# Queueing attention's steps by estimated times instead of one per weight pair, in a two-block transformer kernel

## The reference

```
mod = silu(c) @ w_ada + b_ada            # 2048 -> 12288: six vectors of 2048
h   = modulate(rmsnorm(x), shift_m, scale_m)
dq, dk, dv, q_lat, kv_lat, k_pe = split(h @ w_in)
o_diff = softmax(q1 k1) v - lam * softmax(q2 k2) v      # 8 heads, then an rmsnorm per head
o_mla  = softmax(q_nope k_nope + q_rope k_rope) v       # 8 heads, q and k,v from latents
x = x + gate_m * (concat(o_diff, o_mla) @ w_out)
x = x + gate_f * (relu(modulate(rmsnorm(x), shift_f, scale_f) @ w_ff1)**2 @ w_ff2)
x = rmsnorm(x)
# second block
hn @ w_in_2 -> q,k,v,z of 12 sliding-window heads, of 12 forgetting heads, q,z of 4 memory heads, 3 gates
mk, mv = rmsnorm(mem) @ w_mem_kv
y = sum over branches of sigmoid(gate) * ((attention * silu(z)) @ w_branch)
out = x + y @ w_out_2
```

## Time and profile before

| | before |
|---|---|
| median of 3 runs (lowest, highest) | 2119.35 us (2119.01, 2122.26) |
| the profiled execution: its time | 2116.66 us |
| its span | 2114.6 us |
| PE busy | 1980.5 us, 94% |
| PEld busy | 1631.5 us, 77% |
| DVE busy | 1315.1 us, 62% |
| ACT busy | 941.6 us, 45% |
| instructions | 24917 |

### The profile page before, as it was taken

One profiled execution on the slowest core, in us unless ns is written; L12 is line 12 of the kernel. 1 busy time (PEld: TensorE's weight loads), 2 busy tenths in 40 slices (PEclk: granted clock), 3 DMA queues, 4 the chain that ended last, 5 costly groups with the idle time before them and its releaser, 6 DMA issues. The chain is left out here.

```text
span 2114.6 us, 24917 instructions
## 1 busy us (share of the span) xinstructions
PE 1980.5 (94%) x9272; PEld 1631.5 (77%) x9272; DVE 1315.1 (62%) x2079; ACT 941.6 (45%) x1436; POOL 129.4 (6%) x94
## 2 busy tenths in 40 slices
PE   6798896869899999999999999989999999999999
PEld 3377775548778888888888878889998788888887
DVE  3888776788796555555555556567665555545554
ACT  2554445434544344444434455455444444444442
POOL 0000000002000110110010022010000001101000
PEclk9899998979999999999999999999999999999999
DMA  9997675759797555555555545534544456656654
GB/s 361 382 376 263 241 254 187 249 188 343 273 356 267 194 200 188 190 192 184 191 191 188 186 160 182 188 112 144 164 134 145 132 159 199 189 189 196 192 189 169
DMA packets 128969, 448.83 MB, mean 212 GB/s; under 512 B 14289, under 2 KB 14545, under 8 KB 128337
## 3 DMA queue, kind: packets, MB, share of 16 engines
q1 hardware_dynamic: 124928, 433.74, 60.4%
q0 software_dynamic: 1568, 7.34, 0.9%
q10 hardware_dynamic: 2352, 6.17, 0.8%
HBM read 443.00 MB, written 4.19 MB: 211 GB/s over the span
## 5 line engine op out<-in xcount | busy, mean ns | idle before, releaser
L1724 DVE TENSOR_TENSOR wlo<-raw,whi 128x1024 fp32r<-128x1024 f32 (+4 forms) x554 | 659.4, 1193 | 593.4 <-ACT whi L1511 568.4
L1511 ACT ACTIVATE whi<-raw 128x1024 fp32r<-128x1024 f32 (+4 forms) x554 | 557.0, 1007 | 708.2 <-PE g L1386 638.4
L1381 PE MATMUL g<-whi,lhsA_hi 128*128 128x512 f32 (+4 forms) x1840 | 713.6, 389 | 27.7 <-issue 13.7
L1382 PE MATMUL g<-whi,lhsA_lo 128*128 128x512 f32 (+4 forms) x1840 | 693.5, 379 | 0.0
L1386 PE MATMUL g<-wlo,lhsA_hi 128*128 128x512 f32 (+4 forms) x1840 | 463.7, 374 | 0.0
L1381 PEld LDWEIGHTS g<-whi,lhsA_hi 128*128 128x128 f32 x1840 | 354.9, 193 | 91.9 <-issue 33.1
L1382 PEld LDWEIGHTS g<-whi,lhsA_lo 128*128 128x128 f32 x1840 | 354.9, 193 | 53.3 <-issue 1.7
L1386 PEld LDWEIGHTS g<-wlo,lhsA_hi 128*128 128x128 f32 x1840 | 339.2, 190 | 54.6
L1381 PE MATMUL g<-whi,lhsF_hi 128*128 128x512 f32 x512 | 200.6, 392 | 0.0
L1382 PE MATMUL g<-whi,lhsF_lo 128*128 128x512 f32 x512 | 199.4, 389 | 0.0
L1729 DVE SCALAR_TENSOR_TENSOR raw<-raw,srow 128x1024 f32<-128x1024 f32 x147 | 178.0, 1236 | 19.2 <-DMA raw<-in_w_ada 19.0
(11 more groups left out here) (270 smaller groups left out, 1559.4 us busy)
## 6 DMA issues: line engine op xcount, KB each, us to landing
raw<-in_w_ff SPq DMA_DIRECT2D x182, 512.0 KB, 3.6
raw<-in_w_in SPq DMA_DIRECT2D x161, 512.0 KB, 3.9
raw<-in_w_ada SPq DMA_DIRECT2D x147, 512.0 KB, 5.1
region<-in_w_ff SPq DMA_DIRECT2D x74, 512.0 KB, 4.1
raw<-in_w_out SPq DMA_DIRECT2D x60, 512.0 KB, 5.1
raw<-in_w_in SPq DMA_DIRECT2D x80, 384.0 KB, 3.1
region<-in_w_ada SPq DMA_DIRECT2D x34, 512.0 KB, 5.9
region<-in_w_in SPq DMA_DIRECT2D x15, 512.0 KB, 7.9
```

Of the source, the lines that this page charges most:

```text
L1381: eng.matmul(o, p.xh[:, kk, t * P:t * P + P], h, start=p.first and kk == 0, stop=False)
L1382: eng.matmul(o, p.xl[:, kk, t * P:t * P + P], h, start=False, stop=False)
L1511: eng.activation(p.hi, p.raw, ACT.Copy).then_inc(p.hi_done[0], 1)
L1724: eng.tensor_tensor(p.lo, p.raw, p.hi.bitcast(F32), ALU.subtract).then_inc(p.lo_done[0], 1)
```

## The change

The planner keeps an estimate of the time of each engine (`now`) and of each mark, that is each semaphore value that a step sets (`due`). `TAKES` gives for every kind of step its engine and its us; `step()` adds them. A generator now yields the engine and the marks that its next step waits for; `pump()` lets it go on when those marks are due by the time at which that engine, or PE, is estimated to be (`soon`), and goes round the generators until none moves. Where the planner must have something (`idle`), the generator with the earliest marks goes ahead. The parts of a head are cut by engine: `diff_exp` becomes `diff_max` and `diff_exp`, `diff_mix` becomes `diff_recip`, `diff_scale` and `diff_mix`, `diff_out` loses `diff_sq`; in the same way `soft_max`, `causal_recip` and `x_gain_sq` are split off. The table `ADA_LEFT` is gone: `fill()` queues dots as long as DVE's estimated time at the end of the next one is within `AHEAD` of PE's (3.0 us for the first 64 dots, 3.5 for the next 96, 2.0 for the rest). No instruction is added or dropped in the arithmetic.

```diff
+AHEAD, SLACK = (3.0, 3.5, 2.0), 0.0
...
-ADA_LEFT = {22: 157, 23: 156, 24: 155, 25: 152, 26: 151, 27: 150, 29: 149, 30: 148, 31: 147, 33: 146, 34: 145, 35: 144,
...
+TAKES = {
...
+    "diff_scores": (("pe", 1.15, 6),), "diff_max": (("dve", 0.9, 5),), "diff_exp": (("act", 1.1, 9),),
+    "diff_recip": (("dve", 0.45, 3),), "diff_scale": (("act", 0.45, 5),), "diff_mix": (("dve", 0.46, 5),),
...
+    "mla_scores": (("pe", 1.7, 7),), "soft_max": (("dve", 0.9, 6),), "soft_exp": (("act", 1.1, 8),),
...
+    "store_out": (), "ada_sum": (("dve", 0.6),)}
...
+    due = {landed[n]: t for n, t in dict(c=7.0, cst=9.0, cols=10.0, m0=17.0, m1=20.0, pos=22.0, rows=22.0, x0=26.0, x1=27.0,
+                                         x2=29.0, x3=30.0, xr=0.0, gfin=0.0).items()}
+    now = dict(sp=0.0, dma=9.0, pe=12.0, act=20.0, dve=10.0, pool=0.0)
...
+    def take_time(engine, us, marks, *made):
+
+        now[engine] = max([now[engine]] + [due[m] + 0.07 for m in marks if m in due]) + us
+        for m in made:
+            due[m] = now[engine] + 0.1
 
     def step(*s):
         order.append(s)
+        kind = s[0] + "_pool" if s[0] in ("heads_scale", "add_rows", "y_add") and s[-2] == "pool" else s[0]
+        for engine, us, *at in TAKES.get(kind, ()):
+            take_time(engine, us, marks_in(s[1:]), *[s[i] for i in at])
...
         while all(b.busy for b in ring):
-            pump(1, 4)
+            pump(1, 4, True)
         return pick(ring)
...
+        now["sp"] = max([now["sp"]] + [due[m] for m in raw_free[i]]) + 0.05
+        now["dma"] = max(now["dma"], now["sp"] + 2.0) + n * 0.00282
         raw_free[i] = None
+        due[raw_sem[i], raw_count[i]] = now["dma"]
...
+        take_time("act", 0.1 + 0.00167 * n, [p.landed] + [p.after] * bool(p.after), p.hi_done)
...
         step("ada", x, t, b, k0 // 2, done, b.after)
+        take_time("dve", 1.15, [t], done)
...
     def fill():
-        state["turn"] += 1
-        left = ADA_LEFT.get(state["turn"], 999)
-        while len(adas) > left:
+        while adas:
+            i = state["slot"] % state["ring"]
+            if raw_free[i] is None or (state["hold"] and adas[0][0] >= 20):
+                break
+            issue = max([now["sp"]] + [due[m] for m in raw_free[i]])
+            arrival = max(issue + 2.0, now["dma"]) + 1.45
+            if max(now["dve"], arrival) + 1.2 > now["pe"] + AHEAD[0 if adas[0][0] < 8 else 1 if adas[0][0] < 20 else 2]:
+                break
             ada_next()
 
     bg, started, counts, t_of = deque(), set(), {}, {}
 
-    def pump(n=1, width=2):
+    waiting = {}
+
+    def soon(g, slack):
+
+        engine, marks = waiting.get(id(g)) or ("pe", ())
+        return max([due[m] for m in marks] + [0.0]) <= max(now[engine], now["pe"]) + slack
+
+    def advance(g):
...
+        if w == "end":
+            bg.remove(g)
+        else:
+            waiting[id(g)] = w
+        return len(order) > at or w == "end"
+
+    def pump(n=1, width=2, idle=False):
         for _ in range(n):
             fill()
-            live = 0
-            for g in list(bg):
-                if live < width or g in started:
-                    started.add(g)
-                    live += 1
-                    if next(g, "end") == "end":
-                        bg.remove(g)
+            moved, again = False, True
+            while again:
+                again, live = False, 0
+                for g in list(bg):
+                    if live < width or g in started:
+                        started.add(g)
+                        live += 1
+                        if soon(g, SLACK):
+                            again = advance(g) or again
+                moved = moved or again
+            if idle and not moved:
+                held = [g for g in bg if g in started and waiting.get(id(g))]
+                held.sort(key=lambda g: max([due[m] for m in waiting[id(g)][1]] + [0.0]))
+                for g in held:
+                    if advance(g):
+                        break
...
-                pump(1, 3)
+                pump(1, 3, True)
...
+            if p.native:
+                take_time("pe", 3.43, [p.landed, p.ready, *p.free], tok)
+            else:
+                take_time("pe", 8 * (0.013 + n / 2400), [p.hi_done, p.ready, *p.free])
+                take_time("pe", 4 * (0.013 + n / 2400), [p.lo_done], tok)
...
+        yield "pe", bs[0].after + bs[1].after + [t_of["qT", j], t_of["kT", j]]
         tok = mark("scored")
         step("diff_scores", h, [b.ap for b in bs], bs[0].after + bs[1].after, t_of["qT", j], t_of["kT", j], tok)
-        yield
+        yield "dve", [tok]
+        kms = []
+        for c, b in enumerate(bs):
+            kms.append(mark("negmax"))
+            step("diff_max", c, b.ap, m.ap, [tok] + m.after, kms[c])
         pb = yield from grab(PB)
         for c, b in enumerate(bs):
-            km, ke = mark("negmax"), mark("exp")
-            step("diff_exp", c, b.ap, m.ap, s.ap, pb.ap, tok, m.after, s.after, pb.after, km, ke)
+            yield "act", [kms[c]]
+            ke = mark("exp")
...
-        yield
-        kr, kt = mark("recip"), [(mark("scaled"), mark("mixed")) for _ in range(2)]
...
+        yield "dve", [ke]
+        kr = mark("recip")
+        step("diff_recip", s.ap, ke, kr)
+        kms = []
+        for t in range(2):
+            yield "act", [kr]
+            kms.append(mark("scaled"))
+            step("diff_scale", t, s.ap, pb.ap, kr, kms[t])
+        for t in range(2):
+            yield "dve", [kms[t]]
+            kt = mark("mixed")
+            step("diff_mix", t, s.ap, pb.ap, kms[t], kt)
+        s.release(kt)
...
-        yield
+        yield "act", [tok]
         k = copied(T, tok, pt.ap[:, :], 512, 1.0, *pt.after)
         O = yield from grab(OB)
+        yield "pe", O.after + [k, t_of["dv", j]]
...
-        yield
-        k, ka = mark("odiff"), mark("sqd")
-        step("diff_out", odiff[j][:, :, P * hh:P * hh + P], O.ap, 8 * j + hh, tok, stage, k, ka)
+        yield "dve", [tok]
+        k = mark("odiff")
+        step("diff_out", odiff[j][:, :, P * hh:P * hh + P], O.ap, tok, stage, k)
+        yield "act", [k]
+        ka = mark("sqd")
+        step("diff_sq", O.ap, 8 * j + hh, k, ka)
         O.release(ka)
...
     def diff_end(j):
         yield from need(("ssd", j), 4)
+        yield "dve", [t_of["ssd", j]]
         k = mark("rms")
         step("diff_rsqrt", j, t_of["ssd", j], k)
-        yield
+        yield "dve", [k]
         k2 = mark("odn")
```

More of the change, by code:

```diff
@@ L404, in ada_next @@
             step("ada_sum", c, b, done)
+            due[ada_done[c]] = now["dve"] + 0.1
             b.after = [ada_done[c]]
@@ L950, in reload @@
         step("load_xr", fence())
+        due[landed["xr"]] = max(now["pe"], now["act"], now["dve"]) + 8.0
         x_tok.extend([landed["xr"]] for _ in range(4))
@@ L1024, in final_chunk @@
     def final_chunk(j):
-        for _ in range(2 * (j == 3)):
-            yield
         for p in range(2):
@@ L1296, in turn_y @@
     def turn_y(y, ks, j):
-        for _ in range(2):
-            yield
         for p in range(2):
+            yield "pe", ks
             b = yield from grab(SB)
+            yield "pe", b.after
             tok = turned(b, blocks_of(y.ap, (2 * p * P, 2 * p * P + P)), *ks)
-            yield
+            yield "act", [tok]
             split_from(b, tok, 2, [0.5, 0.5], lhs_y, 4 * j + 2 * p, *stage)
-            yield
         y.release(tok)
@@ L1608, in _ @@
             elif kind == "soft_exp":
-                _, bank, mcol, scol, pb, scale, _, _, s_after, pb_after, km, t = s
-                for m in (km, *s_after, *pb_after):
+                _, bank, mcol, scol, pb, scale, after, km, t = s
+                for m in (km, *after):
                     w.wait_ge(*m)
@@ L1862, in _ @@
                 ins.then_inc(t[0], 1)
-            elif kind == "diff_exp":
-                _, c, bank, mcol, _, _, tok, m_after, _, _, t, _ = s
-                for m in (tok, *m_after):
+            elif kind == "diff_max":
+                _, c, bank, mcol, after, t = s
+                for m in after:
                     w.wait_ge(*m)
```

219 lines of the change are left out of this document (136 added, 83 removed), and 8 rows, old and new, of the table ADA_LEFT.

## The result

| | before | after |
|---|---|---|
| median of 4 runs (lowest, highest) | 2119.18 us (2118.41, 2122.26) | 2053.02 us (2050.08, 2055.5) |
| ratio, 95% interval | | 0.9685 (0.9668 to 0.9701) |
| span of the profiled execution | 2114.6 us | 2048.2 us |
| span less PE's busy time | 134.1 us | 86.5 us |
| granted clock | 0.975 | 0.983 |

The change takes 66 us off. The direction was right and the size was not.

A forecast was written before the change was run, and what follows sets the result against it. PE was taken as the bound, busy 1980.5 of 2114.6 us, leaving 134.1 us idle. Terms +2 - 6 - 20 + 0 - 4 - 2 - 8 = -38 gave 2081 us, range 2060 to 2115.

The forecast's parts named there:

- the clock's price for the heads: Heads in 237 to 404 us: 33 us at the lower clock, called mostly idle time or its wake; -2 us taken.
- -19 for idle time: Heads in 237 to 404 us: of 28.7 us of PE idle, all but 3.7 and 6 us would go.
- I give half back: Second block, 1225 to 1735 us: 14.8 us of waits go, but packed causal heads return half; -8 us.
- +2 to +3.6: Pairs 16 to 46: two to three uncovered dots ahead of low parts for pairs 18 and 19 cost this many us.
- Start: Transposes moved ahead of the first native delay it by 0 to 3.5 us; +2 us taken.
- Heads 4 to 7: 404 to 485 us: dots cluster with head steps on DVE, 86% busy; 0 us taken, bounds -25 to +37.
- fourth case: Pairs 63 to 102: dots ahead of head steps on DVE make it slower, 2136 us; chance 0.10.
- sign of being wrong: The forecast fails if PE's waits for DVE's mixed probabilities or ACT's exps grow; no size given.
- larger gain: Heads in 404 to 485 us gain like the earlier ones, 20 to 40 us more: 2040 to 2062 us; chance 0.08.
- 16 us that the text itself works out for the clock: Heads in 237 to 404 us: at most another 16 us would go if all low-clock time ran high.
- second case: 237 to 485 us: DVE is the bound, gaps only move, the -20 is lost: 2101 us; chance 0.13.
- The third: Planner's estimates are off, such as high parts booked at 0.955 against 1.07 us; waits stay, 2115 to 2120 us; chance 0.03.

The follow-up runs named there:

- e9: Kernel after the change, PE made to wait for 2, 3 or 5 chained GpSimd operations, at lone pairs and in series of 12 pairs: 2330.1 us.
- e6: Kernel after the change, PE made to wait for one GpSimd operation after five lone pairs and each of pairs 600 to 629: 2104.6 us.
- e7: Kernel after the change, memory's arrival and engines' first times re-estimated, mostly later, and the arrival awaited by name: 2045.0 us, ratio 0.965.
- e8: Kernel after the change, dots behind pairs 98 to 103 allowed only within 0.0 us of PE's time in place of 3.5: 2067.6 us, ratio 0.975.
- e11: Kernel after the change, dots 65 to 160 let through within 8.0 us of PE's time in place of 3.5: 2103.3 us, ratio 0.993.
- e13: e7's kernel, steps held until 1.0 us after their marks are estimated due: 2086.0 us; the next run let them through 1.0 us before: 2096.5 us.
- e15: e7's kernel, a high part booked at 1.07 us in place of 0.955: 2058.2 us, ratio 0.971.
- e2: Kernel before the change, with the time estimate added but used for the dots alone, heads moved and cut as before: 2125.8 us, ratio 1.003.
- e5: Kernel after the change, but with as many dots queued behind every pair as the kernel before had by then: 2096.3 us, ratio 0.988.
- e3: Kernel after the change, heads' steps cut as before in place of by engine: 2086.2 us, ratio 0.984.
- e1: Kernel after the change, dots placed by the old table of dots left per turn, which bunched them: 2133.9 us, ratio 1.007.

## Why the prediction was wrong

Its place of the gain was right in every stretch for which it had one, and its size was short by a factor of 1.7: 28 us are missing, 15 of them in PE's busy time (-18.8 for -3.7) and 13 in its idle time (-47.6 for -34.3). By its steps:

- The failing step is the clock's price for the heads. From the earlier trace rows it had 33 us at the lower level, called them "most of it idle time or its wake" and took "-2 for it". Idle time was 1.9 us of it: PE was busy in 30.1 of the 32.0 us that the trace has, and by the two levels half of that, 15 us, was paid. After, 3.2 us at the lower level are left, which makes -13.5 for the -2. With the moved matmuls, some 3 us, this is the 16.6 that busy time lost in pairs 64 to 91. The -19 for idle time there was nearly right (-21.7).
- The same price was left out elsewhere. In the second block PE was busy at the lower level for 12.5 us before and 3.4 after, 4.6 of the 8.0 us that busy time lost there; the other 3.4 have no cause shown. At the feed-forward's start 9.5 us went for 4.3 us of waits; of the 5.2 in busy time 1.7 are the clock (3.4 us at the lower level before, none after) and some 2 the matmuls that moved. Over the whole program PE was busy at the lower level for 76.7 us before and 49.5 after, so 13.6 of the 18.8 us are the clock. e9 shows the price by itself. A wait that the profile shows as 2.3 us costs 4.2. The waits of before were 18.9 / 7 = 2.7 us, nearer to e9's gap than to e6's.
- The second term that was mis-sized is "I give half back" in the second block: nothing was given back. Idle went by 12.3 us of the 17.7, and PE idles 5.4 of 417 us among the packed heads.
- Pairs 16 to 46: the wait of 7.9 us went, and idle time by 8.3 in all. The +2 to +3.6 for dots ahead of the low parts of pairs 18 and 19 didn't come: from pair 16 to 46 PE waits 0.8 and 0.4 us and no more. Busy time fell by 0.7 only: the slow work behind the wait at 46 went, 1.7 us as the text has it, and behind pair 16 more came.
- Start: +4.8 for +2, over its bound of 3.5. The first native is 3.4 us later, which is the bound, and it was taken from PE's transposes alone. What it left out was DVE's queue, where 17.9 us of waiting stand ahead of the first dots. e7 takes that wait away and with it 2 to 3 us by pair 16, which fits, but doesn't show it alone.
- Heads 4 to 7: 0 forecast, +6.5 measured, some 3 of them the matmuls that moved in. Of the fourth case's mechanism the waits ahead of pairs 100 to 103 came as it says (9.2 us, it has 9), and PE's waits for mixed probabilities grew, which the text lists as a sign of being wrong; but the dots in the cluster are worth 6.4 us (e8), not 14.6 and 13 more for their transfers. What is left of the cluster's length is the heads' chain.
- The larger gain had a chance of 0.08 and was thought to be in the cluster. The time lies in its range of 2040 to 2062 by another cause: the clock and the waits everywhere else. With the 16 us that the text itself works out for the clock, in place of 2, the forecast would have been 2067, still above the 2053 measured.
- The second case (DVE bounds the stretch) was wrong for the change, and e11 shows where it comes near to being right: with dots let 8 us behind, DVE is busy 157 of 180 us and 50 us are lost. The third (estimates a little off don't matter) was right that the change does what it says, but not for its reason: e13 to e15 show that an offset of 1 us, or 0.1 in one price, costs 13 to 51 us.

Shown: both halves are needed (e2, e5), the cut by engine (e3), the clock's part (e9, and PE's busy time at the lower level). For e5 the trace shows what the copies stood behind; an order with those fetches moved was not tried. Open are the 5 us of busy time that the clock doesn't explain, how DVE and the transfers share the loss in e1 and e11, and how much of e13 is the heads and how much the place of the dots.

## What to carry to other kernels

Price a wait of TensorE with the slow work behind it: here 0.3 us on top of a wait shown as 1.2 us and 1.9 on top of one shown as 2.3, so that shortening a wait from the second to the first saves 2.7 us and not 1.1. If a planner queues steps by estimated times, all steps of the shared engine, fillers too, must be let in by the same estimate; one half alone gained a third or lost 6 us. Filler held back must be paid by its deadline (25 us in e8). Bound a moved step on every engine and queue that it uses, not only on the one that was waiting: in e5 fetches on SP held up a high part, and that a copy.
